# A two-block layer kernel on one core: the first weight block multiplied as the input's chunks arrive, the key blocks ordered by token tile, the compressed logits placed later, and the edges of the first attention reordered

## The reference, cut to what matters

```
h = rmsnorm(x, norm_pre); proj = h @ w_in
z, xbc, dt, q, k, v, z_sb, gates = split(proj)
xs, bm, cm = split(silu(causal_conv(xbc)));  y = ssd_scan(xs, softplus(dt + bias), a, bm, cm)
y_ssd = gated_norm(y, z) @ w_ssd
o = stick_breaking(q, k, v):  logits q k^T, w = sigmoid(l) * prod of sigmoid(-l) after it, w @ v
y_sb = (o * silu(z_sb)) @ w_sb
x1 = x + rmsnorm((g_ssd * y_ssd + g_sb * y_sb) @ w_out, norm_post)
h2 = rms_norm(x1, norm_mix);  proj2 = h2 @ w_in_2     # q, compressed, selected and window k and v, HGRN parts
p_cmp = masked_softmax(q @ compress(k)^T);  o_nsa = gates * (p_cmp @ vc, selected, window)
x2 = x1 + concat(o_nsa, o_hgrn) @ w_out_2
out = x2 + (silu(gate) * up) @ w_down
```

## Time and profile before

| | before |
|---|---|
| median of 3 runs | 1399.78 us (1398.46 to 1401.15) |
| the profiled execution, own time | 1397.56 us |
| its span | 1395.8 us |
| PE, PEld busy | 1366.4 us (98%), 1131.8 us (81%) |
| DVE, ACT busy | 753.2 us (54%), 608.8 us (44%) |
| granted TensorE clock, mean | 0.996 |
| DMA | 121.27 MB, mean 87 GB/s |

### The profile page before, as it was taken

How to read it: one execution, slowest core, us unless ns; L and a number is a source line. 1 busy time by engine, 2 the same in 40 slices (tenths; PEclk the granted TensorE clock), 3 DMA queues, 4 the chain that set the end, 5 groups by cost and what they waited for, 6 DMA issues and landing times. The chain is left out here.

```text
span 1395.8 us, 18000 instructions
## 1 busy us (share of the span) xinstructions
PE 1366.4 (98%) x7055; PEld 1131.8 (81%) x7055; DVE 753.2 (54%) x1180; ACT 608.8 (44%) x1128; POOL 54.3 (4%) x38
## 2 busy tenths in 40 slices
PE   9999999999999999999998999999999999999999
PEld 7878778877888888887787777878898888888887
DVE  4875544456666554445557677668554433443333
ACT  5553333457777533223425467763343212321221
POOL 0015310000000000000010000000000000000000
PEclk9999999999999999999999999999999999999999
DMA  4222122242111244222441100101422332223223
GB/s 153 87 76 91 62 76 93 89 131 82 31 62 61 86 170 147 91 91 73 154 131 47 60 28 19 32 0 55 156 77 91 106 106 91 91 92 102 95 89 106
DMA packets 35349, 121.27 MB, mean 87 GB/s; under 512 B 3908, under 2 KB 5188, under 8 KB 35010
## 3 DMA queue, kind: packets, MB, share of 16 engines
q1 hardware_dynamic: 34690, 119.07, 26.0%
q10 hardware_dynamic: 576, 1.05, 0.3%
HBM read 112.77 MB, written 4.19 MB: 84 GB/s over the span
## 5 line engine op out<-in xcount | busy, mean ns | idle before, releaser
L845 PE MATMUL bank<-a_hi,whi 128*128 128x512 f32 (+1 forms) x880 | 346.3, 393 | 1.4 <-DVE arena L2108 0.9
L845 PE MATMUL bank<-a_hi,wlo 128*128 128x512 f32 (+1 forms) x880 | 336.9, 383 | 0.0
L845 PE MATMUL bank<-a_lo,whi 128*128 128x512 f32 (+1 forms) x880 | 336.4, 382 | 0.0
L1268 ACT ACTIVATE whi<-wraw 128x1024 fp32r<-128x1024 f32 x194 | 197.1, 1046 | 193.2 <-PE bank L845 169.3
L1620 DVE TENSOR_TENSOR wlo<-wraw,whi 128x1024 fp32r<-128x1024 f32 x194 | 238.2, 1239 | 61.6 <-ACT whi L1268 56.9
L845 PEld LDWEIGHTS bank<-a_hi,whi 128*128 128x128 f32 x880 | 165.8, 188 | 32.9 <-ACT whi L1268 2.0
L845 PEld LDWEIGHTS bank<-a_hi,wlo 128*128 128x128 f32 x880 | 165.5, 188 | 32.6
L845 PE MATMUL bank<-arena 128*128 128x128 f32 (+5 forms) x1332 | 185.1, 285 | 6.8 <-DVE arena L1982 2.6
L845 PEld LDWEIGHTS bank<-a_lo,whi 128*128 128x128 f32 x880 | 165.9, 188 | 30.6 <-issue 1.4
L845 PEld LDWEIGHTS bank<-arena 128*128 128x128 f32 (+1 forms) x1332 | 165.4, 191 | 18.7 <-issue 6.4
L845 PE MATMUL bank<-whi,a_hi 128*128 128x512 f32 x288 | 115.8, 402 | 2.4 <-DVE wlo L1620 2.3
(11 more groups left out here) (257 smaller groups left out, 1718.5 us busy)
## 6 DMA issues: line engine op xcount, KB each, us to landing
wraw<-in_wblk SPq DMA_DIRECT2D x190, 512.0 KB, 3.7
arena<-in_x SPq DMA_DIRECT2D x4, 512.0 KB, 6.1
arena<-in_x SPq DMA_DIRECT2D x1, 2048.0 KB, 7.6
spill<-arena SPq DMA_DIRECT2D x4, 512.0 KB, 7.7
arena<-spill SPq DMA_DIRECT2D x1, 2048.0 KB, 9.4
out<-arena SPq DMA_DIRECT2D x8, 256.0 KB, 2.6
arena<-arena SPq DMA_DIRECT2D x2, 896.0 KB
arena<-in_w1k SPq DMA_DIRECT2D x1, 1024.0 KB, 7.2
```

The lines of the kernel that those rows point to most:

```text
L845: return nc.tensor.matmul(o, lhsT, rhs, start=start, stop=stop, **kw)
L1268: A(whi[n % 2][:, cols], wraw[i][:, 0:cols.stop - cols.start], ACT.Copy).then_inc(s_hi, 1)
```

## The change

The arithmetic stays the same; each matmul has its operands of before, and one small activation is added. Steps and waits move:

1. Block 0 is rounded among the chunks, and is multiplied in halves of the rows (`parts`): chunks 0 to 3 for both tiles, then chunks 4 to 7. The `dt` product comes behind block 0, and the other dt steps one block later.
2. Two slices of the first k block stand ahead of the weave with the SSD steps.
3. The gate tiles take the banks in the order 1, 2, 0; z_sb waits for the attention only in bank 3; unit 0 no longer waits for the last reading of v, which moves to head 1; DVE takes the differences of v ahead of the stack; ACT touches Sigmoid once behind its stack; the second shifted copy of v is issued behind the next piece of weights.
4. Blocks 45, 46, 47 and their norms and turns are reordered by token tile, with triggers of their own.
5. Four slices of block 52 stand ahead of the compressed logits. They wait for the queries alone; the keys are waited for one step later, in the first turn.

```diff
-    steps.append(("small", "dt", tile("dt_t", 0)))
     for j in range(XC // 2):
         block_ = feature("w_in", [(XBC0 + 256 * j, 256)], [("xbc", 2 * j), ("xbc", 2 * j + 1)], "AA")
-        if j == 1:
+        if j == 0:
+            blocks[0]["parts"] = [(j_, k, whole[0]) for a in (0, NK // 2) for j_ in range(2) for k in range(a, a + NK // 2)]
+            block_.append(("small", "dt", tile("dt_t", 0)))
+        if j == 2:
             block_ = weave(block_, [("dt", i) for i in range(3)])
         steps += block_
-        if j == 0:
+        if j == 1:
             steps.append(("smallturn", "dt", tile("dt", 0)))
...
-        if j == 2:
+        if j == 3:
             steps.append(("ssd_decay",))
...
-    steps += weave([("ssd", c, part) for c in range(NT) for part in range(5)], kq)
+    steps += kq[:2] + weave([("ssd", c, part) for c in range(NT) for part in range(5)], kq[2:])
...
-    steps += o[6] + N("out1", 2) + A("out1", 2) + o[7][:1] + N("mix", 2) + o[7][1:] + turns("mix", 1)
     kv = token("w_in_2", KS0, "kv", 0, "A")
     kv = [kv[:SLICES], kv[SLICES:]]
-    steps += N("out1", 3) + A("mix", 2) + A("out1", 3) + kv[0][:2] + N("mix", 3) + kv[0][2:4] + turns("mix", 2) + A("mix", 3)
-    steps += kv[1][:4] + turns("mix", 3) + kv[0][4:] + kv[1][4:]
+    steps += o[6] + o[7] + turns("mix", 1) + N("out1", 2) + kv[0][:1] + A("out1", 2) + kv[0][1:2] + N("mix", 2)
+    steps += N("out1", 3) + A("mix", 2) + kv[0][2:4] + A("out1", 3) + kv[1][:3] + turns("mix", 2) + N("mix", 3) + A("mix", 3)
+    steps += kv[1][3:4] + kv[0][4:6] + turns("mix", 3) + kv[1][4:6] + kv[0][6:] + kv[1][6:]
+    last_, first_, second_ = o[7][0][1], kv[0][0][1], kv[1][0][1]
+    triggers[first_] = [(last_, 4), (last_, 5)], [(last_, 5), (last_, 5)]
+    triggers[second_] = [(first_, 0), (first_, 1)], [(first_, 0), (first_, 1)]
+    triggers[second_ + 1] = [(first_, 7), (second_, 6)], [(second_, 6), (second_, 7)]
...
-    steps += weave(cmps, token("w_in_2", HI0, "hi", 0, "A"))
+    hi = token("w_in_2", HI0, "hi", 0, "A")
+    steps += hi[:4] + weave(cmps, hi[4:])
...
-              "gate": (0, 1, 2), "y_ssd": (0, 1, 2)}
+              "gate": (1, 2, 0), "y_ssd": (1, 2, 0)}
...
-SHIFTS = [block_of("v") + 4, block_of("v") + 5]
+SHIFTS = [(block_of("v") + 4, 0), (block_of("v") + 5, 1)]
...
-                if TILES[g][0] == "z_sb":
+                if TILES[g][0] == "z_sb" and BANK[g] == BANKS_STICK[1]:
                     pe.wait_ge(s_o, SH)
...
-                if s == (2 if b["form"] == "feature" and len(b["parts"]) == 2 * NK else 1):
+                if s == (4 if n == 0 else 2 if b["form"] == "feature" and len(b["parts"]) == 2 * NK else 1):
...
                     if qt == 0:
                         pe.wait_ge(s_vcd, 1)
-                        pe.wait_ge(*ended(tile_of("turn_qk", 5)))
+                        pe.wait_ge(*ended(tile_of("turn_qk", 3)))
...
                     pe.wait_ge(s_cp, qt + 1)
+                    if qt == 0:
+                        pe.wait_ge(*ended(tile_of("turn_qk", 5)))
...
                     if u == 0:
-                        pe.wait_ge(*end_sem("v"))
                         need_split(max(SPLITS.index(x) for x in SPLITS if x[:2] == ("turn", "y")) + 1)
...
                         pe.wait_ge(s_dv, 1 + h // 8)
+                        if h == 1:
+                            pe.wait_ge(*end_sem("v"))
...
                 if s == ("chunk", 0, tile_of("x_t", 0)):
+                    round_weights(0, 0)
+                if s == ("chunk", NK // 2, tile_of("x_t", NK // 2)):
+                    round_weights(0, 1)
+                if s == ("gemm", 0, 0):
                     round_small("dt")
...
                     for i in range(3):
                         stack(0, i)
+                    A(unit_root, unit, ACT.Sigmoid)
...
+                if s == ("chunk", 0, tile_of("x_t", 0)):
+                    rest_of_weights(0, 0)
+                if s == ("chunk", NK // 2, tile_of("x_t", NK // 2)):
+                    rest_of_weights(0, 1)
...
                     dve.wait_ge(s_kz, 1)
-                    for i in range(2):
-                        stack(0, i)
                     for half in range(2):
                         link(v.memset(v_before[half][0:1, 0, :], 0.0))
                     for t in range(NT):
                         steps_of_values(0, t)
+                    for i in range(2):
+                        stack(0, i)
```

More of the change, by code:

```diff
@@ L790, in _ @@
                     sp.dma_start(wraw[i][:, 0:cols.stop - cols.start], dram["wblk"][n][:, cols]).then_inc(s_w[i], 16)
-                    if i == 0 and n in SHIFTS:
-                        half = SHIFTS.index(n)
+                    if (n, i) in SHIFTS:
+                        half = SHIFTS.index((n, i))
                         src, dst = vt[:, :, 512 * half:512 * half + 512], v_before[half]
@@ L1507, in _ @@
                 if s == ("chunk", 0, tile_of("x_t", 0)):
+                    round_weights(0, 0)
+                if s == ("chunk", NK // 2, tile_of("x_t", NK // 2)):
+                    round_weights(0, 1)
+                if s == ("gemm", 0, 0):
                     round_small("dt")
                 if s[0] == "small":
-                    if s[1] == "dt":
-                        for i in range(2):
-                            round_weights(0, i)
                     act.wait_ge(s_tile, DONE[s[2]])
@@ L2117, in _ @@
                                            f32(a_hi[:, c, :]), ALU.mult, ALU.subtract).then_inc(s_split, 1)
-                if s == ("chunk", 0, tile_of("x_t", 0)):
+                if s == ("gemm", 0, 0):
                     rest_of_small("dt")
@@ L2138, in _ @@
                     rest_of_small("gates")
-                if s[0] == "small":
-                    if s[1] == "dt":
-                        for i in range(2):
-                            rest_of_weights(0, i)
                 if s[0] == "dt":
```

## The result

| | before | changed |
|---|---|---|
| median, same chip (4 runs each) | 1399.12 us (1397.88 to 1401.15) | 1382.11 us (1381.39 to 1382.47) |
| ratio, 95% interval | | 0.9876 (0.9859 to 0.9894) |
| profiled execution, own time / span | 1397.56 / 1395.8 us | 1382.09 / 1380.3 us |
| granted clock, mean | 0.996 | 1.0 |

A forecast was written before the change was run, and what follows sets the result against it. TensorE, busy 98% of the span, was taken as the bound. Gains of 1.9 + 1.4 + 3.5 + 0.9 + 2.6 + 6.5 = 16.8 us off the median of 1399.78 gave 1383.0 us, range 1380 to 1389.

The forecast's parts named there:

- Start: Kernel start: block 0 multiplied at DVE's pace ahead of dt, gain 1.9 us, bounds 0.3 to 2.3.
- First SSD scores: Wait of 1.37 us on DVE's last convolution gets two slices in front: gain 1.4 us, at least 1.0.
- z_sb: Wait of 0.88 us for the last attention output, on banks the attention doesn't use: gain 0.9 us, at least 0.3.
- head of the attention: First attention: PE's waits of 0.89, 1.14 and 1.59 us go, gain 3.5 us, lower bound 1.0.
- The cap of 3.6 at the attention: Head of the first attention: PE's three waits make 3.6 us and cap the gain there.
- Keys' blocks: Blocks 45 to 47: 2.3 wait plus 1.9 lost clock less 1.4 new waits, less 0.2 restart: gain 2.6 us.
- Compressed logits: Wait of 3.47 us and the low clock behind it both go: gain 6.5 us, bounds 3.5 to 6.9.
- Given back later: Later stages up to the compressed logits wait for DMAs, half the gain lost: about 1391 us, chance 0.05.
- one of the prediction's own signs of being wrong: Prediction is wrong if waits of over 1 us show in stages that the change doesn't touch.
- The rival by the clock in the keys' blocks: Clock falls again in the keys' blocks, 1.9 us stay lost: 1384.9 us, chance 0.12.
- The slower rival: Attention gate tiles wait for bank readings, deciding from 0.31 us a unit; at 0.5 it gives 1415 us; chance 0.03.
- The sign "a clock of 1.00 in every 5 us": Whole kernel: a granted clock of 1.00 in every 5 us would show the forecast right.

The follow-up runs named there:

- run 9: The changed kernel once more, with nothing altered: 1382.82 us, ratio 0.9887.
- Run 7: The changed kernel with the order and triggers around the keys' blocks undone: 1382.79 us, ratio 0.9889.
- run 1: The kernel before with only four slices of block 52 ahead of the compressed logits, which wait for the fourth qkturn: 1392.65 us against 1398.11.
- run 2: The kernel before with 15 extra full matmuls, their product unread, just ahead of the wait of 3.47 us: 1396.09 us against 1398.11.
- run 11: The kernel before with only the piece of weights issued ahead of the second shifted copy of v: 1396.13 us against 1398.04.
- run 8: The changed kernel with the copies of the residual and two loads of constants issued one block earlier: 1381.24 us, ratio 0.9873.
- run 6: The changed kernel with the second shifted copy of v issued ahead of the piece of weights again: 1386.19 us, ratio 0.9914.
- run 10: The changed kernel with the start, the slices ahead of the SSD scores with ssd_decay's place, and z_sb's rule of banks undone: 1386.86 us, ratio 0.9918.
- run 5: The changed kernel without the early sigmoid on one column: 1384.18 us, ratio 0.9894.

## Why the forecast was right, and where it was off

The forecast of 1383.0 us stands 0.9 above the median of 1382.11, and 1380.8 for the profiled execution 1.3 below its 1382.09. Five of the six terms are right in mechanism and within 0.4 us. That the sum came as near as it did is in part luck: three terms that were too small (by 0.9 together) make up for the start and the keys' blocks, which were too large by as much. Point by point:

- *Start* (1.9). Right. 1.67 in the first trace, where the input's second tile landed late (PE's wait for it ends at 9.52, against 9.27 in run 9, as before the change); 1.85 with an equal landing. The first full matmul came at 15.59, not 15.2, and at 15.15 to 15.93 in the others with this start, as the input landed.
- *First SSD scores* (1.4), *z_sb* (0.9), *head of the attention* (3.5). Right in mechanism and each 0.2 to 0.4 too small. I took the idle times of the rows as the price. Between the same matmuls a wait cost more than its idle time (1.70 for 1.37, 1.13 for 0.88, 3.91 for 3.62). The cap of 3.6 at the attention ("The three waits make 3.6") was wrong for that reason.
- *Keys' blocks* (2.6; measured 1.86). The mis-sized term, by 0.7 us. The two new waits make 1.33 us, against 1.4 forecast, with the sizes changed over (0.51 and 0.82 for 0.9 and 0.5). The step that failed is the term of 1.9 for the lost clock in the sum "2.3 + 1.9 - 1.4 = 2.8". Run 7 and three others have this stretch at full clock and within 0.1 us just as long, with a third wait of 0.9 that the slow clock had hidden in the earlier trace rows. The account at full clock fits: 0.61 + 2.29 + 0.91 = 3.81 of waits before, 0.61 + 0.51 + 0.82 = 1.94 now, 1.87 less. In the place of the 1.9 the sum should have had that third wait, 0.9. The text had asked of each stall what is late next, and did not ask it of the slow clock.
- *Compressed logits* (6.5; measured 6.60). Right; run 1 gave the same alone, and run 2 split it: 3.04 of it went with the clock. The size holds against the profiled execution that it was read from. Against run 11's trace, with the shorter fall, the same seam of run 1 would have gained 5.2, and the medians of run 1 differ by 5.5.
- *Given back later* (chance 0.05, by way of "the spill of the residual and the weights beside it"). It happened in part: 1.39 us between blocks 49 and 52 in one execution and 1.01 in another. Beside the wait for the gelu, a wait of 0.35 us for DVE's b_lo in the kernel before is 0.50 in both. The wait of 1.01 us is one of the prediction's own signs of being wrong, a wait of over 1 us in a stage that the change doesn't touch. Runs 7 and 8 showed the path: PE is 10.3 us early, the copies begin only 7.7 us earlier, they fill the DMA engines, a piece of weights lands late, and ACT's reading of the first qn tile stands in order behind that piece's rounding. As a case it was priced too high, at half of the sum; as a term of the sum, some 1.0 to 1.4, it was missing, and it is nearly the whole distance of the profiled executions.
- *The rival by the clock in the keys' blocks* did not come about: the clock was 1.00 there in both traces of the changed kernel. *The slower rival* neither: blocks 23 to 29 take 126.10 us with the new ring and took 126.19 before, where 0.31 us a unit would have decided; all fourteen traces lie between 126.06 and 126.20, so the ring shows no effect. The sign "a clock of 1.00 in every 5 us" held in the first trace of the changed kernel up to the last microseconds of the span, and not in run 9.

The excess of the median gain (17.0) over the profiled one (15.5) is the kernel before's: its profiled execution lay 1.6 us under its median. Its 39 runs beside the experiments spread from 1396.0 to 1402.57 us with their mean granted clock: 1396.0 to 1396.2 at 0.999, 1397.2 to 1399.6 at 0.996, 1400.1 to 1401.3 at 0.994 and 1402.57 at 0.992. The eight executions of the changed kernel have 0.998 to 1.0 and lie between 1381.39 and 1383.26.

## What to carry to other kernels

A stall or a slow clock is worth only the time up to the next wait: ask what is late next before booking the lost clock as a gain. Edits at one seam don't add up. At the attention's head the transfer's new place alone gained 1.62 us, and the three other edits 2.29 on top of it; without it they gained nothing (run 6). When an engine comes earlier to a later stage, list what doesn't: here a row of copies that came less early than PE took back 1.0 to 1.4 of the 1.9 us that the keys' blocks had gained, and issuing them in an idle stretch undid that.

## What the runs showed of the hardware that was not expected

- The same wait does not always have the low clock behind it. A wait of 1.52 us at the head of the second attention is in all fourteen profiled executions; in four of them (runs 1, 6, 9, 10) a fall followed it, and the stretch from block 54 to block 55 took 1.5 to 1.6 us more; in ten none did. A wait of 1.71 us (1.70 in some), 20 us later, stands in all fourteen too, and none of them has a fall behind it. The wait of 2.29 us had a fall behind it in one of five. The wait of 3.47 us had one in both traces that have it, but at a price of 3.0 us in the kernel before and 1.6 in run 11. The third wait at the first attention had one at 2.07 and at 3.04 us, none at 1.29, 1.45 and 1.59. So the length of a wait alone does not decide. The Trainium skill ("TensorE: Matmul & The Clock Gate", section "What's actually happening") ties the clock to how busy the array has been lately; the traces fit that it is idleness that brings it down, and no row tells why one execution of the same order falls and the next does not.
- A single wait cost 0.25 to 0.35 us more between the same matmuls than the idle time in its row (0.88 and 1.13; 1.37 and 1.70).
- A table load of ACT took 1.28 us and was not preceded or followed by idle time: in run 5 it begins 0.01 us behind one activation, and the next begins 0.02 behind it.
